# A kernel of two transformer blocks: the first two bunches' expert weights in the order of x's columns, and a 21st slot for expert weights

## The chip, the cores and the metric

The kernel runs on one core of a Trainium2 chip. The metric is the device time of one execution in microseconds, the median of three runs. The engines named here are TensorE (PE, matmuls; PEld is its weight load), VectorE (DVE), ScalarE (ACT), GpSimd (POOL) and SyncE (SP). SyncE issues nearly all loads from device memory to on-chip memory (SBUF), in the order of its program, into one queue that 16 DMA engines serve.

## The reference

Input is x, 256 tokens of 1024 float32 values. The first block is a hybrid of three attention mixers (sliding window with sinks, dilated groups, latent attention), an output projection, a layer norm, and a mixture of experts:

```python
g_logits = x @ w_rg + b_rg                  # 4 groups, the best one is taken
e_logits = (x @ w_re[grp]) + b_re[grp]      # 8 experts in each group, the best two are taken
gate = softmax(top2) * p_grp
y[t] = sum over its 2 experts e: gate * (silu(x[t] @ w_gate[e]) * (x[t] @ w_up[e])) @ w_down[e]
x = layer_norm(ALPHA * x + y, ln2_g, ln2_b)
```

There are 32 experts. `w_gate[e]` and `w_up[e]` are 1024 x 256, `w_down[e]` is 256 x 1024, each 1 MB in float32, so the experts' weights are 96 MB and all of them are read. Behind this come two layers of a second block (differential, grouped-query and memory attention, gates, an output projection and norms), whose weights are 1024 wide too.

The sum over the 1024 rows of `w_gate[e]` may be taken in any order, as long as row i of the weights meets column i of x. This is the freedom that the two layouts below use.

## The kernel before, in words

**Stages.** The input projections and mixers of the first block run until about 177 us of the profile, then the first layer norm and the router until about 201 us, the experts until about 440 us, and the second block behind them.

**Bunches of experts.** The experts go in 8 bunches of 4 (`AT_ONCE`). In each, every expert has 32 places (`PLACES`) for tokens, so the bunch has 128. A 256 x 128 matrix of ones and zeros, `places2`, says which token stands in which place. TensorE gathers the tokens with it: `gather_half` (line 1198) makes for each of 8 chunks k a 128 x 128 result, x's columns of chunk k (stationary) times `places2` (moving), summed over the two halves of the tokens. In the profile a float32 matmul leaves two records, so a half gather is 16 records and a whole one 32. ScalarE copies each half to `q_c` (line 1613). `gate_up` (line 1235 on, matmuls at 1246) then multiplies 32 places of each expert with that expert's gate and up weights, 256 + 256 columns at once, the four experts beside each other; its first half takes chunks 0 to 3, its second chunks 4 to 7. The sigmoid is made by ACT (1619) and DVE (2114 to 2117, `hidden_done`), the hidden values are turned (1224), and `down` (1260) multiplies with the down weights. `add_back` (1232) adds the weighed results to each token's row.

The order on TensorE is: half gather of bunch 0, first half of gate/up of bunch 0, second half gather, second half of gate/up, the residual term (1320, 8 records of 512 columns, only in bunch 0), the whole gather of bunch 1, `down` of bunch 0, `add_back`, gate/up of bunch 1, gather of bunch 2, `down` of bunch 1, and so on.

**Layout of the weights.** Each bunch has 12 items of 1 MB, in this order: four with rows of chunks 0 to 3 of gate and up of its four experts, four with chunks 4 to 7, and four with the down weights. Before the change partition p holds rows 8p to 8p+7 of the gate weights (`(p k) n -> p k n`), so chunk k is every eighth row, and the load moves runs of 4 KB. The gather must then take every eighth column of x as its stationary operand. The down weights are loaded as runs of 8 KB.

**Slots.** An expert item goes into one of 20 slots of 1 MB: the 12 of the tile `ring`, and 8 that lie in other tiles once these are no longer used (`beyond_ring`). `FIRST_SLOTS` is the order in which they are first filled. Four of them (`ONCE`) are filled once only, the others come back at the end of the list each time. `free_for_experts` (from line 707) is what SyncE waits for ahead of each load: for a first filling, the last use by the mixers, the layer norm or the router; later, the use of the item that lies in the slot. `gu_half` b+1 is the end of the first half of gate/up in bunch b, `gu_ready` b+1 that of the second, and `y_ready` 2b+2 the end of its `down`. In bunches 0 to 2 the items and slots are:

- bunch 0: K_C, TILES_MID, BIAS_HIGH, BIAS_LOW, PROBS_T, 2, 3, 4 (gate/up), 0, 1, 6, 9 (down)
- bunch 1: 7, 10, 5, 8, 11, MIX_T, LN_ROWS, X_T (gate/up), then K_C (free at `gu_half` 1), PROBS_T, 2, 3 (at `gu_ready` 1) (down)
- bunch 2: 4 (at `gu_ready` 1), 0, 1, 6, 9 (at `y_ready` 2), 7, 10, 5 (at `gu_half` 2) (gate/up), 8 (at `gu_half` 2), 11, MIX_T, X_T (at `gu_ready` 2) (down)

The last bunch does not use slots 0 to 3; the first weights of the second block (`mem_k0`, `mem_v0`, then `w_in` items 0, 1, 2) are loaded into slots 0 to 4 behind the experts by line 685, in runs of 1 KB. Every load waits in the same queue as the experts' weights.

**Other users of the tiles.** `v_nat` holds the values of two mixers, and `v_c` those of the third; the last product that reads them is the one before the output projection of the first block, `LAST_OUT_1`. During the experts, columns 0 to 1023 of `v_nat` hold the bunch's results (`y_e`). Columns 1024 to 2047 are scratch for the squares of the memory rows (`mem_junk`). `probs` holds the router's values during the experts, in its first columns (`rcol`).

Of the kernel before, what the change touches and what calls it, by code (L numbers as in the profile page):

```python
# [15 lines left out]
P = 128  # L16
# [110 lines left out]
ITEM = {name: n for n, name in enumerate(ITEMS)}  # L127


BIAS_LOW, BIAS_HIGH, PROBS_T, MIX_T, X_T, K_C, TILES_MID, LN_ROWS = range(RING, RING + 8)  # L130
FIRST_SLOTS = (K_C, TILES_MID, BIAS_HIGH, BIAS_LOW, PROBS_T, 2, 3, 4, 0, 1, 6, 9, 7, 10, 5, 8, 11, MIX_T, LN_ROWS, X_T)
ONCE = (TILES_MID, BIAS_HIGH, BIAS_LOW, LN_ROWS)
NEXT_LAYERS = (0, 1, 2, 3)
EXPERT_RING = len(FIRST_SLOTS)
PER_BUNCH = 12


def expert_slots():
# [259 lines left out]
def build(nc, ins, out):  # L398
    ctx = ExitStack()
    with ctx:  # L400
        def sb(name, shape, dt=F32):
            return ctx.enter_context(nc.sbuf_tensor(name, shape, dt))
# [17 lines left out]
        const = sb("const", [P, N_CONST])  # L420
        x_nat = sb("x_nat", [P, 2 * D])
        tiles = sb("tiles", [P, TILES2 * T])
        v_nat = sb("v_nat", [P, 2048])
        q_c = sb("q_c", [P, C_HEADS * T])
        k_c = sb("k_c", [P, C_HEADS * T])
        v_c = sb("v_c", [P, 1024])
        bias = sb("bias", [P, BIAS_HEADS * T])
        probs = sb("probs", [P, 2 * 1152])
        probsT = sb("probsT", [P, 4 * 512])
# [46 lines left out]
        def as_f32(a):  # L476
# [40 lines left out]
        more_g, more_u, more_d = (ring[:, SLOT * k:SLOT * k + SLOT] for k in (9, 10, 11))  # L517
        beyond_ring = {BIAS_LOW: bias[:, 0:2048], BIAS_HIGH: bias[:, 2048:4096], PROBS_T: probsT[:, :],
                       MIX_T: mixT[:, :], X_T: xT[:, :], K_C: k_c[:, :], TILES_MID: tiles[:, 2048:4096],
                       LN_ROWS: tiles[:, 4096:6144]}  # L520

        def expert_slot(n):

# [29 lines left out]
        bucket_sb, rel_sb = probsT[0:N_BUCKETS, 0:VALS + 1], probsT[0:N_BUCKETS, 384:384 + BIAS_HEADS]  # L553
        unseen_sb, bias_sb = probsT[0:BIAS_HEADS, 512:512 + VALS], probsT[0:BIAS_HEADS, 1024:1024 + VALS]
        rope_s = q_c[:, 0:512]
        mem_junk = v_nat[:, 1024:2048]
        rope_a = q_c[:, 7 * T:8 * T]

        def sq_tile(n):
# [11 lines left out]
        def rcol(n):  # L571
            a = rt[0]
            rt[0] += n
            assert rt[0] <= 2048
            return probs[:, a:a + n]

        logitT_sb = rcol(T)
# [74 lines left out]
        def _(sp):  # L652
# [51 lines left out]
            def free_for_experts(n):  # L704

                k = slot_of(n)
                earlier = [m for m in range(FIRST_EXPERT, n) if slot_of(m) == k]
                if earlier:
                    sp.wait_ge(*expert_done(earlier[-1]))
                elif k < MIXERS_RING:  # L710
                    used_up(max(m for m in range(FIRST_EXPERT) if slot_of(m) == k))
                elif k < RING - 1:
                    owners = {UNIT_OWNER[u] for u in range(units_before(OPENING[1])) if u % UNITS // 2 == (k - 5) % 3}
                    sp.wait_ge(p_ready, max(max(users(n)) for n in owners) + 1)
                elif k == K_C:
                    sp.wait_ge(scores, s_first(STEP[("C", 0, C_HEADS - 1)]) + 1)
                elif k == TILES_MID:
                    sp.wait_ge(scores, s_first(STEP[("B", 0, B_HEADS - 1)]) + 3)
                elif k in (BIAS_LOW, BIAS_HIGH):
                    sp.wait_ge(maxed, STEP[("B", 0, B_HEADS - 1)] + 1)  # L720
                elif k == PROBS_T:
                    sp.wait_ge(o_ready, LAST_OUT_1)
                elif k == LN_ROWS:
                    sp.wait_ge(ln_done, 2)
                elif k == X_T:
                    sp.wait_ge(p_ready, JOB[("logit",)] + 1)
                else:
                    sp.wait_ge(p_ready, JOB[("y1", 3, 1)] + 1)

            def load_expert(n):  # L730

                free_for_experts(n)
                b, j = divmod(n - FIRST_EXPERT, PER_BUNCH)
                e = b * AT_ONCE + j % AT_ONCE
                to = expert_slot(n)
                if j < GATE_UP:
                    half = j // AT_ONCE
                    for m, name in enumerate(("w_expert_gate", "w_expert_up")):
                        w = ins[name][0, e].rearrange("(p k) n -> p k n", p=P)
                        sp.dma_start(to[:, SLOT // 2 * m:SLOT // 2 * m + SLOT // 2].rearrange("p (k n) -> p k n", n=DE),  # L740
                                     w[:, 4 * half:4 * half + 4, :]).then_inc(loaded[slot_of(n)], 16)
                else:
                    sp.dma_start(to, ins["w_expert_down"][0, e].rearrange("(p k) n -> p (k n)", p=P)
                                 ).then_inc(loaded[slot_of(n)], 16)
# [99 lines left out]
        def _(pe):  # L844
# [350 lines left out]
                                mm = pe.matmul(o, v, pt[:, T:2 * T], start=False, stop=last)  # L1195
                mm.then_inc(o_ready, 1)

            def gather_half(half):

                dst = bank(4 + half)  # L1200
                for c in range(4):
                    k = 4 * half + c
                    for tt in range(2):
                        mm = pe.matmul(dst[:, P * c:P * c + P],  # L1204
                                       x2[:, tt, :].rearrange("p (q k) -> p k q", k=KC)[:, k, :],
                                       places2[:, tt, :], start=(tt == 0), stop=(tt == 1))
                mm.then_inc(gathered_ready, 1)

            def turn_weighed():
# [2 lines left out]
                    mm = pe.transpose(bank(7)[:, P * tt:P * tt + P], weighed2[:, tt, :], ident)  # L1212
                mm.then_inc(back_ready, 1)

            def gather():

                for half in range(2):
                    gather_half(half)
                turn_weighed()

            def turn_hidden(dst):
# [48 lines left out]
            def more_bunch(n):  # L1270

                i = n + BUNCHES
                pe.wait_ge(placed, i + 1)
                gather()
                pe.wait_ge(gathered_out, 2 * i + 2)
                for e in range(AT_ONCE):
                    pe.wait_ge(more_in, n * (32 * AT_ONCE) + 32 * (e + 1))
# [28 lines left out]
            def experts():  # L1306
# [1 line left out]
                pe.wait_ge(p_dve, taken(JOB[("rank",)]))  # L1308
                pe.wait_ge(setup, 2)
                pe.wait_ge(placed, 1)  # L1310
                gather_half(0)
                for b in range(BUNCHES):
                    gate_up(b, 0)
                    if b == 0:
                        gather_half(1)
                        turn_weighed()
                    gate_up(b, 1)
                    if b == 0:
                        for m in range(4):
                            pe.matmul(bank(m), diagonal[:, P * (m // 2):P * (m // 2) + P],  # L1320
                                      x2[:, m // 2, 512 * (m % 2):512 * (m % 2) + 512],
                                      start=True, stop=False, skip_group_check=True)
                    if b + 1 < BUNCHES:
                        if b > MEM_AT:
                            pe.wait_ge(memT_out, b - MEM_AT)
                        pe.wait_ge(placed, b + 2)
                        gather()
                    else:
                        pe.wait_ge(routed, 1)
                        some = pe.value_load(flags[0:1, 112:113], min_val=0, max_val=1)  # L1330
                    pe.wait_ge(hidden_done, b + 1)
                    turn_hidden(bank(6))
                    pe.wait_ge(hT_out, b + 1)
                    pe.wait_ge(back_out, min(b + 2, BUNCHES))
                    pe.wait_ge(gathered_out, 2 * min(b + 2, BUNCHES))
                    down(b)
                    if MEM_AT <= b < MEM_AT + KC // 2:
                        turn_memory(b - MEM_AT)
                    pe.wait_ge(y0_out, b + 1)
                    pe.wait_ge(y1_out, b + 1)  # L1340
                    add_back(backs[b % 2])
# [1024 lines left out]
```

## Time and profile before

| what | before |
|---|---|
| median of 3 runs | 768.28 us (767.44 to 771.92) |
| the profiled execution | 766.16 us |
| its span, first to last instruction | 764.4 us |
| TensorE busy | 681.9 us, 89% |
| VectorE busy | 368.5 us, 48% |
| ScalarE busy | 324.1 us, 42% |
| DMA | 167.8 MB, mean 220 GB/s |
| mean granted TensorE clock | 0.962 of 2.4 GHz |

The page cuts the span into 40 slices of 19.1 us. These are its rows for the DMA engines:

```
DMA  9967331498667999999999919007263080073301
GB/s 281 339 196 245 111 111 56 127 358 313 247 269 255 416 407 415 413 411 415 410 415 415 322 61 299 29 1 248 83 220 111 1 258 19 1 223 109 111 1 56
```

A digit is the busy share of a slice in tenths. The expert stage is slices 11 to 23, and in its greater part the queue is full at 407 to 416 GB/s. A share over 1 appears where packets of several queues overlap. All times below are of this one execution, from its first instruction.

### The profile page before, as it was taken

To read this page: it belongs to the slowest core of one execution; us is meant where nothing else is said; L and a number is where in the kernel's file an instruction comes from. 1 tells how busy PE (TensorE), PEld (TensorE's weight loads), DVE (VectorE), ACT (ScalarE), POOL (GpSimd) and SP (SyncE) were. 2 spreads that over 40 slices of the span, in tenths; PEclk is the share of its full clock that TensorE was granted. 3 is DMA by queue.
4 is the path that set the end of the run, shared out by engine and by line. 5 is a ranking of instruction groups with operands and counts; after the bars stand their busy time and mean duration, and the time that the engine had idled before them with its cause. 6 is when DMAs were issued, how large, how long until landed. Compare 5 with 4: busy or idle time off the path is not lost.

```text
span 764.4 us, 11653 instructions
## 1 busy us (share of the span) xinstructions
PE 681.9 (89%) x4580; PEld 524.3 (69%) x4582; DVE 368.5 (48%) x813; ACT 324.1 (42%) x759; POOL 16.8 (2%) x31
## 2 busy tenths in 40 slices
PE   6989999996599999697887789999979999999986
PEld 4968998695363555253452378888859898888876
DVE  1633657445431232021110376678775566787743
ACT  2555665421000112120110243578875545788742
POOL 6001000000000000000000000000000000000000
PEclk9999999998599999899999899999999999999999
DMA  9967331498667999999999919007263080073301
GB/s 281 339 196 245 111 111 56 127 358 313 247 269 255 416 407 415 413 411 415 410 415 415 322 61 299 29 1 248 83 220 111 1 258 19 1 223 109 111 1 56
DMA packets 82328, 167.80 MB, mean 220 GB/s; under 512 B 4238, under 2 KB 59264, under 8 KB 78176
## 3 DMA queue, kind: packets, MB, share of 16 engines
q1 hardware_dynamic: 79984, 160.88, 58.1%
q0 software_dynamic: 2160, 6.07, 2.4%
q8 instruction: 39, 0.64, 0.4%
q14 instruction: 17, 0.14, 0.1%
q10 hardware_dynamic: 128, 0.08, 0.0%
HBM read 165.93 MB, written 1.07 MB: 218 GB/s over the span
## 4 chain that ended last, share of the span: by engine, by line
PE 70%; SPq 13%; ACT 5%; DVE 5%; DMA 5%; issue 2%; ACTq 0%; DVEq 0%
PE psum L850 13%; PE psum L852 11%; PE psum L851 11%; SPq L740 9%; PE psum L1204 5%; PE psum L1246 4%; PE psum L893 3%; PE psum L1144 3%; PE psum L1191 2%; DMA ring<-in_w_expert_up_dram 2%; PE psum L1260 2%; SPq L685 2%; DMA ring<-in_w_in_dram 2%; PE psum L1103 2%; PE psum L1232 1%
## 5 line engine op out<-in xcount | busy, mean ns | idle before, releaser
L850 PE MATMUL psum<-a_high,w_high 128*128 128x256 f32 x512 | 150.9, 295 | 2.1 <-ACT q_c L1471 1.3
L851 PE MATMUL psum<-x_low,w_high 128*128 128x256 f32 x512 | 144.6, 283 | 0.0
L852 PE MATMUL psum<-a_high,w_low 128*128 128x256 f32 x512 | 144.6, 283 | 0.0
L2186 DVE TENSOR_TENSOR w_low<-ring,w_high 128x1024 fp32r<-128x1024 f32 (+1 forms) x79 | 111.2, 1422 | 25.1 <-ACT w_high L1571 25.1
L850 PEld LDWEIGHTS psum<-a_high,w_high 128*128 128x128 f32 x512 | 97.7, 191 | 13.9 <-issue 4.7
L1571 ACT ACTIVATE w_high<-ring 128x1024 fp32r<-128x1024 f32 (+1 forms) x79 | 95.9, 1219 | 10.7 <-DMA ring<-in_w_in_dram 7.4
L851 PEld LDWEIGHTS psum<-x_low,w_high 128*128 128x128 f32 x512 | 97.8, 191 | 0.4
L852 PEld LDWEIGHTS psum<-a_high,w_low 128*128 128x128 f32 x512 | 97.8, 191 | 0.0
L1246 PE MATMUL psum<-ring,q_c 128*32 128x512 f32 x368 | 60.7, 654 | 14.6 <-DMA ring<-in_w_expert_up_dram 10.0
L850 PE MATMUL psum<-w_high,a_high 128*128 128x256 f32 x240 | 69.6, 290 | 0.0
L851 PE MATMUL psum<-w_low,a_high 128*128 128x256 f32 x240 | 68.5, 285 | 0.0
L1204 PEld LDWEIGHTS psum<-tiles,x_nat 128*128 128x128 f32 x256 | 61.7, 334 | 8.4 <-issue 8.3
L1204 PE MATMUL psum<-tiles,x_nat 128*128 128x128 f32 x256 | 63.2, 407 | 2.1 <-DVE tiles L2103 2.1
L852 PE MATMUL psum<-w_high,mix_low 128*128 128x256 f32 x192 | 54.8, 286 | 0.0
L2114 DVE TENSOR_SCALAR tiles<-tiles 128x256 f32<-128x256 f32 x8 | 2.3, 292 | 104.8 <-ACT tiles L1619 104.8
L850 PEld LDWEIGHTS psum<-w_high,a_high 128*128 128x128 f32 x240 | 46.7, 195 | 3.2 <-issue 2.3
L1246 PEld LDWEIGHTS psum<-ring,q_c 128*32 128x32 f32 x368 | 15.8, 118 | 46.1 <-issue 46.1
L851 PEld LDWEIGHTS psum<-w_low,a_high 128*128 128x128 f32 x240 | 46.7, 195 | 0.0
L1619 ACT ACTIVATE tiles<-psum 128x256 f32<-128x256 f32 x8 | 3.1, 383 | 100.8 <-PE psum L1246 100.8
L1613 ACT ACTIVATE q_c<-psum 128x512 f32<-128x512 f32 x16 | 9.6, 597 | 69.4 <-PE psum L1204 69.4
L852 PEld LDWEIGHTS psum<-w_high,mix_low 128*128 128x128 f32 x192 | 37.4, 195 | 0.0
L1144 PE MATMUL psum<-const,probs 128*128 128x128 f32 x200 | 31.7, 280 | 4.6 <-DVE probs L1972 2.4
(334 smaller groups left out, 1168.4 us busy)
## 6 DMA issues: line engine op xcount, KB each, us to landing
ring<-in_w_in_dram SPq DMA_DIRECT2D x36, 1024.0 KB, 8.6
ring<-in_w_expert_gate_dram SPq DMA_DIRECT2D x46, 512.0 KB, 14.5
ring<-in_w_expert_up_dram SPq DMA_DIRECT2D x46, 512.0 KB, 15.6
ring<-in_w_expert_down_dram SPq DMA_DIRECT2D x22, 1024.0 KB, 17.4
ring<-in_w_out_dram SPq DMA_DIRECT2D x12, 1024.0 KB, 5.2
ring<-in_w_mem_kv_dram SPq DMA_DIRECT2D x4, 1024.0 KB, 16.8
mixT<-in_w_expert_down_dram SPq DMA_DIRECT2D x3, 1024.0 KB, 18.7
xT<-in_w_expert_down_dram SPq DMA_DIRECT2D x3, 1024.0 KB, 20.6
```

The costliest lines, as they stand in the source:

```text
L685: sp.dma_start(slots[:, s, :, 0:src.shape[2]], src).then_inc(loaded[s], 16)
L740: sp.dma_start(to[:, SLOT // 2 * m:SLOT // 2 * m + SLOT // 2].rearrange("p (k n) -> p k n", n=DE), w[:, 4 * half:4 * half + 4, :]).then_in ...
L850: pe.matmul(dst, left[0], right[0], start=first, stop=False)
L851: pe.matmul(dst, left[0], right[1], start=False, stop=False)
L852: return pe.matmul(dst, left[1], right[0], start=False, stop=last)
L893: mm = pe.matmul(dst, src[:, k, P * tt:P * tt + P], w[:, k, a:b], start=(k == 0), stop=(k == KC - 1))
L1103: mm = pe.matmul(banks[m][:, T * tt:T * tt + T], q[:, P * tt:P * tt + P], k, start=True, stop=True)
L1144: mm = pe.transpose(dst[:, P * c:P * c + P], pr[:, a:a + P], ident)
L1204: mm = pe.matmul(dst[:, P * c:P * c + P], x2[:, tt, :].rearrange("p (q k) -> p k q", k=KC)[:, k, :], places2[:, tt, :], start=(tt == 0), s ...
L1246: mm = pe.matmul(bank(6)[PLACES * e:PLACES * e + PLACES, :], gathered2[b % 2][:, k, PLACES * e:PLACES * e + PLACES], w, start=(k == 0), st ...
L1571: act.activation(split_like_raw(n)[0], raw_of(n), ACT.Copy).then_inc(highs, 1)
L2186: dve.tensor_tensor(w_l, raw_of(n), as_f32(w_h), ALU.subtract).then_inc(lows, 1)
```

## The change

Three things change together.

1. `IN_ORDER = 2`: in bunches 0 and 1, partition p of chunk k holds row 128k + p of the gate and up weights (`(k p) n -> p k n`), so these loads move runs of 1 KB. The gather of these bunches reads `x4`, in which chunk k is 128 neighbouring columns of x. Bunches 2 to 7 and the rounds for more than 32 tokens of an expert keep the old layout. The down weights keep theirs.
2. `v_nat` and `v_c` become parts of one tile, `values`, and its columns 1024 to 3071 are a 21st slot, `V_TOP`. It stands sixth in `FIRST_SLOTS`, behind PROBS_T, waits for the same semaphore as PROBS_T at its first filling, and comes back like the others.
3. `mem_junk` moves from `v_nat` to columns 1152 to 2175 of `probs`, and the router's columns are held below 1152.

With the new list the slots of the first bunches are:

- bunch 0: K_C, TILES_MID, BIAS_HIGH, BIAS_LOW, PROBS_T, V_TOP, 2, 3 (gate/up), 4, 0, 1, 6 (down)
- bunch 1: 9, 7, 10, 5, 8, 11, MIX_T, LN_ROWS (gate/up), X_T, K_C (at `gu_half` 1), PROBS_T, V_TOP (at `gu_ready` 1) (down)
- bunch 2: 2, 3 (at `gu_ready` 1), 4, 0, 1, 6 (at `y_ready` 2), 9, 7 (at `gu_half` 2) (gate/up), 10, 5 (at `gu_half` 2), 8, 11 (at `gu_ready` 2) (down)

```diff
-BIAS_LOW, BIAS_HIGH, PROBS_T, MIX_T, X_T, K_C, TILES_MID, LN_ROWS = range(RING, RING + 8)
-FIRST_SLOTS = (K_C, TILES_MID, BIAS_HIGH, BIAS_LOW, PROBS_T, 2, 3, 4, 0, 1, 6, 9, 7, 10, 5, 8, 11, MIX_T, LN_ROWS, X_T)
+BIAS_LOW, BIAS_HIGH, PROBS_T, MIX_T, X_T, K_C, TILES_MID, LN_ROWS, V_TOP = range(RING, RING + 9)
+FIRST_SLOTS = (K_C, TILES_MID, BIAS_HIGH, BIAS_LOW, PROBS_T, V_TOP, 2, 3, 4, 0, 1, 6, 9, 7, 10, 5, 8, 11, MIX_T, LN_ROWS, X_T)
...
+IN_ORDER = 2
...
-        v_nat = sb("v_nat", [P, 2048])
+        values = sb("values", [P, 3072])
+        v_nat, v_c = values[:, 0:2048], values[:, 2048:3072]
...
-        v_c = sb("v_c", [P, 1024])
...
-                       LN_ROWS: tiles[:, 4096:6144]}
+                       LN_ROWS: tiles[:, 4096:6144], V_TOP: values[:, 1024:3072]}
...
-        mem_junk = v_nat[:, 1024:2048]
+        mem_junk = probs[:, 1152:2176]
...
-            assert rt[0] <= 2048
+            assert rt[0] <= 1152
...
-                elif k == PROBS_T:
+                elif k in (PROBS_T, V_TOP):
                     sp.wait_ge(o_ready, LAST_OUT_1)
...
-                        w = ins[name][0, e].rearrange("(p k) n -> p k n", p=P)
+                        w = ins[name][0, e].rearrange("(k p) n -> p k n" if b < IN_ORDER else "(p k) n -> p k n", p=P)
                         sp.dma_start(to[:, SLOT // 2 * m:SLOT // 2 * m + SLOT // 2].rearrange("p (k n) -> p k n", n=DE),
                                      w[:, 4 * half:4 * half + 4, :]).then_inc(loaded[slot_of(n)], 16)
...
-            def gather_half(half):
+            def gather_half(b, half):
...
-                        mm = pe.matmul(dst[:, P * c:P * c + P],
-                                       x2[:, tt, :].rearrange("p (q k) -> p k q", k=KC)[:, k, :],
-                                       places2[:, tt, :], start=(tt == 0), stop=(tt == 1))
+                        x = x4[:, tt] if b < IN_ORDER else x2[:, tt, :].rearrange("p (q k) -> p k q", k=KC)
+                        mm = pe.matmul(dst[:, P * c:P * c + P], x[:, k, :], places2[:, tt, :],
+                                       start=(tt == 0), stop=(tt == 1))
...
-            def gather():
+            def gather(b):
...
-                gather()
+                gather(BUNCHES)
...
-                gather_half(0)
+                gather_half(0, 0)
...
-                        gather_half(1)
+                        gather_half(0, 1)
...
-                        gather()
+                        gather(b + 1)
```

## Rows read from the trace of the kernel before

**Rows 1.** Windows: span, PE, PEld, DVE, ACT, POOL busy, clock, DMA share, GB/s

```profile
200.00:210.00 10.00, 7.98 (x36) 4.91 (x40) 1.12 (x6) 0.60 (x1) 0.00 (x0) 0.50 0.27 107
...
250.00:420.00 170.00, 143.02 (x847) 76.06 (x847) 29.33 (x61) 23.18 (x49) 0.00 (x0) 0.95 1.02 413
...
236.00:244.00 8.00, 7.09 (x44) 2.50 (x44) 0.69 (x1) 0.00 (x0) 0.00 (x0) 1.00 0.81 244
...
28.00:48.00 20.00, 17.96 (x129) 15.73 (x128) 11.67 (x33) 11.61 (x20) 0.00 (x0) 1.00 1.10 349
...
12.00:16.00 4.00, 4.00 (x10) 3.19 (x11) 2.58 (x3) 1.01 (x2) 0.00 (x0) 1.00 1.14 210
```

**Rows 2.** Chain of waits, in order of time: start us, us, what

```profile
206.20 5.82 PE psum L1246 x32
...
216.71 3.64 PE psum L1246 x32
...
223.98 7.50 PE psum L1204 x32
...
247.65 7.83 PE psum L1204 x32
...
424.73 13.23 DMA ring<-in_w_in_dram
...
440.30 1.22 DVE small L1993 x2
```

**Rows 3.** SyncE's issues in order of time: start us, us, what

```profile
154.19 0.33 SPq L740 DMA_DIRECT2D probsT<-in_w_expert_gate_dram  x1
...
159.91 15.42 SPq L743 DMA_DIRECT2D ring<-in_w_expert_down_dram  x4
...
190.51 0.33 SPq L740 DMA_DIRECT2D xT<-in_w_expert_gate_dram  x1
...
212.09 0.33 SPq L743 DMA_DIRECT2D k_c<-in_w_expert_down_dram  x1
220.41 0.33 SPq L743 DMA_DIRECT2D probsT<-in_w_expert_down_dram  x1
...
236.13 0.33 SPq L740 DMA_DIRECT2D ring<-in_w_expert_gate_dram  x1
...
244.28 0.33 SPq L740 DMA_DIRECT2D ring<-in_w_expert_gate_dram  x1
```

**Rows 4.** Windows of 2 us about the pauses of the DMA engines

```profile
172.00:174.00 2.00, 2.00 (x19) 2.00 (x19) 1.81 (x5) 0.29 (x1) 0.00 (x0) 1.00 0.23 94
...
202.00:204.00 2.00, 2.00 (x10) 2.00 (x10) 0.00 (x0) 0.00 (x0) 0.00 (x0) 0.50 0.33 127
...
232.00:234.00 2.00, 1.57 (x16) 0.55 (x20) 1.04 (x5) 0.38 (x2) 0.00 (x0) 1.00 0.09 37
...
236.00:238.00 2.00, 1.09 (x7) 0.57 (x4) 0.69 (x1) 0.00 (x0) 0.00 (x0) 1.00 0.34 86
```

**Rows 5.** TensorE in order of time: gathers (L1204) and line 1018

```profile
201.33 4.18 PE L1204 MATMUL psum<-tiles,x_nat 128*128 128x128 f32 x16 [2.12 <-DVE tiles L2103]
...
211.95 4.08 PE L1204 MATMUL psum<-tiles,x_nat 128*128 128x128 f32 x16
...
223.82 7.65 PE L1204 MATMUL psum<-tiles,x_nat 128*128 128x128 f32 x32
...
448.31 2.02 PE L1018 MATMUL psum<-diagonal,x_nat 128*128 128x128 f32 x16 [1.55 <-ACT diagonal L1562]
```

**Rows 6.** Weight loads of these lines: ns min/median/max, first and last start

```profile
L1204 PEld LDWEIGHTS psum<-tiles,x_nat x256: 312/335/338, 201.3 to 397.0; 128*128 128x128 f32 x128
...
L1018 PEld LDWEIGHTS psum<-diagonal,x_nat x64: 186/192/192, 448.3 to 607.2; 128*128 128x128 f32 x64
```

**Rows 7.** TensorE in order of time: the router's rank matmuls, five in a row

```profile
196.90 0.60 PE L1009 MATMUL psum<-probs,const 128*128 128x32 f32 x2 [5.47 <-DVE probs L2048]
...
198.60 0.61 PE L1013 MATMUL psum<-probs 128*128 128x32 f32 x2
```

More of the change, by code:

```diff
@@ L1213, in turn_weighed @@
                 mm.then_inc(back_ready, 1)
-            def gather():
+            def gather(b):
                 for half in range(2):
-                    gather_half(half)
+                    gather_half(b, half)
                 turn_weighed()
```

## The prediction, made before the changed kernel was run

> **What bounds the kernel now.** I read four views, in this order: windows by stage, the chain of waits, SyncE's issues in order of time, and TensorE's matmuls in order of time. The expert stage runs from 201 to 440 us, and nothing that the change does shortens a stage before or behind it. So the question is what ends this one.
>
> From 250 to 420 us the DMA engines are never free: share 1.02, 413 GB/s [rows 1]. Before 240 us they often are: share 0.27 from 200 to 210 us. TensorE is the full engine there. The chain says the same in order of time [rows 2]: matmuls from the start of the stage, and at its end the load queue. The last link is a 1 MB load of `w_in`, issued at 424.73 and landed at 437.98 us; its split and the second layer norm follow (440.30). It stands behind all expert weights in one queue. So the stage ends when the queue becomes continuous plus the bytes still to come, and an idle microsecond recovered before that comes off the end.
>
> What ends each idle piece is a slot that comes free [rows 3]. SyncE issues into the last of the 20 slots at 190.51 us, then stands until `gu_half` 1 (212.09), `gu_ready` 1 (220.41), `y_ready` 2 (236.13) and `gu_half` 2 (244.28). The engines run dry at 202.7 (0.33 of a 2 us window) and 232.2 us (0.09), and are filled again at 237.3 (0.34 of the window is used), a microsecond behind the issue [rows 4]. From there they don't stop. TensorE sets all four releases, and before 232 us it spends 4.18 + 4.08 + 7.65 us on gathers [rows 5].
>
> **The change part by part.**
>
> *Gathers of bunches 0 and 1.* The stationary operand becomes 128 neighbouring columns of x in place of every eighth. At the full clock, 16 records (8 matmuls) take 4.08 us now and 32 take 7.65. The same shape from neighbouring columns of the same tile is line 1018's: 16 records in 2.02 us [rows 5], so 32 in about 3.9; its weight load takes 192 ns where the gather's takes 335 [rows 6]. Saved: 2.06 us in the second half of bunch 0, 3.75 us in bunch 1. The first half of bunch 0 runs at 1.2 GHz (granted 0.50 from 200 to 210 us [rows 1]) and takes 4.18/16 = 0.261 us a record. Contiguous ones would take there between 0.213 us, the pace of the rank matmuls ((198.60 − 196.90)/8 [rows 7]), and twice line 1018's 0.126, so the saving is 0.1 to 0.8 us; I take 0.5, the middle. Half of that goes again, because the gate/up matmuls behind then run longer in the slow stretch: 0.25.
>
> The Trainium skill (TensorE: Matmul & The Clock Gate, "Wait — 56ns, not 53.3ns?") gives 106.7 ns cold and 55.6 ns warm for 128 columns, and its page FP8 and Floating Point Precision counts four passes for fp32. An estimate from the two is 3.4 us for the first half and 3.6 us for 16 matmuls, and by it the sum would be 0.7 us larger. No row here shows so quick a gather, and line 1018's pace stands.
>
> Is something else late next? The sigmoid of bunch 0 takes 4.2 us from the end of gate/up to `hidden_done`; TensorE has 3.6 us of residual and 3.9 us of gather over it, so it stays hidden. If it did not, what it exceeds them by would come back. The copies to `q_c` stay behind each half gather. So `gu_half` 1 comes 0.25 us earlier, `gu_ready` 1 2.3 us (0.25 + 2.06), `y_ready` 2 6.05 us (2.3 + 3.75): 230.1 us. `gu_half` 2 moves as far, to 238.2.
>
> *The 21st slot* waits for the same semaphore as PROBS_T (154.19 us [rows 3]), so no new wait stands in SyncE's queue. Every item behind it takes the slot one place earlier. At 190.51 us the ninth item of bunch 1 goes out instead of the eighth, and the load that `y_ready` 2 releases is one further on. One MB at 413 GB/s [rows 1] is 2.54 us less behind that point.
>
> *1 KB runs for 4 KB in the 16 gate/up items of bunches 0 and 1.* A full queue of 1 KB runs moves 349 GB/s, one of expert weights 413 [rows 1]: 3.00 against 2.54 us per MB, 7.4 us in all. Where do they fall? From 154.2 us: four gate/up items (12.0), one down item (2.5), two more (5.1), to 173.8 us. Today the queue runs empty near 172.5 us [rows 4], while SyncE stands within its four down issues until 175.3 us, for a slot of the mixers [rows 3]; that pause is filled. Then a down and a gate/up item (5.5), six gate/up items from 177.4 (18.0), LN_ROWS (3.0), X_T as a down item (2.5): empty at about 204 us, 202.7 before. The next release is at 212, so the 7.4 us are paid where nobody waits, with 8 to spare. Bunch 1's last gate/up item lands near 202 us and is wanted at 238. SyncE issues two loads per item as before.
>
> *From 212 us on.* K_C and the memory rows last to 218; `gu_ready` 1 at 218.1 releases four items, done at about 229.8; `y_ready` 2 at 230.1 four more, flowing from 231.3; `gu_half` 2 (238.2) comes before those are through (241.5). Later releases lead by as much as today. The continuous stretch starts at 231.3 instead of 237.3.
>
> *The rest costs nothing.* The values keep their places within one tile; the squares' scratch moves to columns of `probs` that the router does not use. The third `w_in` load's slot is now freed by the last down product, which in today's trace ends near 430.5 us, where SyncE comes to that load; the critical one is the second.
>
> **Sum.** 6.0 (earlier start) + 2.54 (one MB fewer) = 8.5 us. All of it passes to the end, because TensorE needs 23.7 us from gather to gather (223.98 to 247.65 [rows 2]) and the queue 12 × 2.54 = 30.5 us per bunch. The span goes from 764.4 to 755.9 us, the profiled run from 766.2 to 757.7; the median of the runs, 768.28, is 2.1 above that run: 759.8 us.
>
> Bounds: the first gather's 0.1 to 0.8, and the poor rate of a burst, 244 GB/s at share 0.81 over 236 to 244 us [rows 1], some 2 us that a queue already running may not lose, or may lose once more: 6.5 to 10.5 us saved, 757.8 to 761.8.
>
> **Rivals.**
>
> *The clock comes back later.* It returns to 2.4 GHz after about 9 us of work, inside the gate/up matmuls that take 5.82 us on the chain, against 3.64 for as many at the full clock [rows 2]. A shorter gather brings the copy's gap forward. Should the return come after these matmuls, they take 2 × 3.64 = 7.3 (1.4 more), and some of the next gather is slow (0.6): 761.8 us. For it: the return lies close behind the changed work. Against: TensorE is busy on both sides of a 0.65 us gap, as now. 0.17.
>
> *The layout does not speed the gather*, because the load is bound by something else. Only the slot is left: 765.7 us. Against it, line 1018 reads the very same tile. 0.07.
>
> *1 KB runs go far slower (the slower side).* Its place is the queue from 154 to 231 us. The lowest row with such runs has 210 GB/s, among small loads (12 to 16 us [rows 1]), and 4 KB bursts fall to 244. Twelve gate/up items lie behind 154.2 us, with five down items (12.7) and then six more MB (15.2) before `y_ready` 2. The queue is late from 4.1 us per item on, 256 GB/s. At 210 GB/s it is 5.0: 154.2 + 60 + 27.9 = 242.1, 10.8 us behind, and the net is 2.3 us slower, 770.6; at 190 GB/s 777. Against: 20 us at 349. 0.06, half of it past +1%.
>
> The Trainium skill (DMA: Bandwidth & Descriptors, "Why small descriptors are slow (HBM only)") counts a fixed 3 cycles per packet, by which an estimate for 1 KB against 4 KB is 7% more time. The rows show 18%, and they are used; by either the queue is idle at 212 us.
>
> *More than forecast:* the burst loses nothing and the gather has its best bound: 757.5 us. 0.10.
>
> **Chances.** Forecast 0.60, rivals as given. About 1%, 7.7 us, is what a measurement of this kernel can tell from no change, so the line is 760.6 us and runs through the forecast's own range. Faster by over 1%: 0.42 of the forecast's 0.60, and the 0.10: 0.52. Slower 0.03, within 1% 0.45. The range is 756.8 to 765.5: it takes in the bounds, the late clock and, nearly, the slot alone.
>
> **What would show it.** Right: gather records at 0.126 us in the first two bunches and 0.245 in the others; issues near 218 and 230 us; a full queue from 231 us; the second `w_in` load landed near 429.5, and all that follows 8 to 9 us early. Wrong: a queue still full at 212 us, 1 KB items below 300 GB/s, 1.2 GHz beyond 212 us, or TensorE waiting for bunch 1's weights.

## The result, and the profile after

| what | before | changed |
|---|---|---|
| median, first comparison | 767.74 us (10 runs) | 759.57 us (10 runs) |
| ratio, first comparison | | 0.9888, 95% interval 0.9862 to 0.9915 |
| ratio, second comparison (kernel a1, the same code) | | 0.9916, 95% interval 0.9885 to 0.9947 |
| span of the profiled execution | 764.4 us | 760.2 us; a1: 754.8 us |

The kernel became about 1% faster, 6.4 to 8.6 us by the two comparisons. The forecast was 8.5 us and 759.8 us. The prediction's line between "faster by over 1%" and "within 1%", 760.6 us, runs between the two measured medians (759.57 and 760.96 us): the two comparisons fall on either side of it. The first profile of the changed kernel alone would mislead: its span is only 4.2 us shorter. The second one is 9.6 us shorter. So two profiles of the same code are read here beside the one of before. Lines of the changed kernel have moved by one or two: the gather is L1206 (before L1204), `gate_up` L1247 (L1246), `down` L1261 (L1260), the residual L1321 (L1320).

First the chain of waits of the changed kernel's first profile, from the first gather on, and the end of its expert stage (columns: start us, us, what):

```profile
204.95 3.77 PE psum L1206 x16
...
209.39 5.57 PE psum L1247 x32
214.96 2.00 PE psum L1206 x16
...
217.63 3.64 PE psum L1247 x32
221.27 3.63 PE psum L1321 x8
224.90 3.58 PE psum L1206 x32
...
229.43 3.69 PE psum L1261 x32
...
244.65 7.83 PE psum L1206 x32
...
424.50 3.67 PE psum L1233 x8
428.17 3.20 issue
431.37 1.07 PE psum L1352 x3
```

The gathers of bunches 0 and 1 answer to [rows 5]: 2.00 us in place of 4.08, 3.58 in place of 7.5 on the chain, and bunch 2's is 7.83 as ever. But the stage begins at 204.95 us, 3.6 us later than before, and near its end stand 3.20 us in which TensorE waits for nothing that the profile shows. Neither was in the prediction.

The same stretch in a1, TensorE in order of time:

```profile
201.45 3.76 PE L1206 MATMUL psum<-tiles,x_nat 128*128 128x128 f32 x16 [2.12 <-DVE tiles L2104]
...
211.83 2.05 PE L1206 MATMUL psum<-tiles,x_nat 128*128 128x128 f32 x16
...
221.68 3.73 PE L1206 MATMUL psum<-tiles,x_nat 128*128 128x128 f32 x32
```

Here the stage begins where it began before (201.33 [rows 5]). SyncE's issues in a1, which answer to [rows 3]:

```profile
211.97 0.34 SPq L744 DMA_DIRECT2D k_c<-in_w_expert_down_dram  x1
218.27 0.33 SPq L744 DMA_DIRECT2D probsT<-in_w_expert_down_dram  x1
...
230.08 0.33 SPq L741 DMA_DIRECT2D ring<-in_w_expert_gate_dram  x1
...
238.22 0.33 SPq L741 DMA_DIRECT2D ring<-in_w_expert_gate_dram  x1
```

Forecast were about 211.8, 218.1, 230.1 and 238.2 us. And the windows of a1 (columns as in [rows 1]):

```profile
206.00:208.00 2.00, 2.00 (x12) 0.48 (x16) 0.00 (x0) 0.00 (x0) 0.00 (x0) 0.50 0.06 16
212.00:214.00 2.00, 2.00 (x18) 1.86 (x18) 0.00 (x0) 0.08 (x1) 0.71 (x1) 1.00 0.58 74
...
226.00:228.00 2.00, 1.62 (x16) 0.55 (x20) 0.99 (x5) 0.32 (x2) 0.00 (x0) 1.00 0.92 231
228.00:230.00 2.00, 2.00 (x20) 0.39 (x12) 0.00 (x0) 0.60 (x1) 0.00 (x0) 1.00 0.98 356
230.00:232.00 2.00, 1.09 (x6) 0.63 (x4) 0.69 (x1) 0.00 (x0) 0.00 (x0) 1.00 0.91 348
232.00:234.00 2.00, 2.00 (x6) 0.81 (x5) 0.00 (x0) 0.00 (x0) 0.00 (x0) 1.00 0.87 219
...
180.00:200.00 20.00, 9.95 (x44) 7.13 (x44) 9.41 (x41) 2.88 (x7) 0.00 (x0) 0.67 1.10 350
...
250.00:420.00 170.00, 143.99 (x834) 71.50 (x838) 30.84 (x62) 22.82 (x50) 0.00 (x0) 0.91 1.02 411
```

The queue with 1 KB runs moves 350 GB/s from 180 to 200 us and is empty at 206.1 us. (Its share of 1.10 is that of one queue alone, 110.1% for SyncE's, and it was 109.8% from 28 to 48 us in [rows 1]: with 1 KB runs a share over 1 does not take several queues.) It is busy again from 212.8 us, and the pause that the old kernel had from 232 to 237 us [rows 4] is gone. The critical `w_in` load was used at 437.98 us in the kernel before. In a1, ScalarE's line for it and DVE's for the layer norm behind it are:

```profile
428.12 1.06 ACT L1572 ACTIVATE w_high<-ring 128x1024 fp32r<-128x1024 f32 x1 [0.88 <-DMA ring<-in_w_in_dram]
...
430.35 1.29 DVE L1994 BATCH_NORM_STATS2 small<-psum 128x6 f32<-128x512 f32 x2
```

Both are 9.9 us earlier than before (437.98 and 440.21 there). But not all of it passes on. Two things must be done before TensorE can turn the normed rows (the scaled transposes, L1018 before, L1019 now): the layer norm behind the `w_in` load, and TensorE's own work, which is the last bunch's `down` and `add_back`, the first matmuls of the second block (L986) and those of line 894. Before, TensorE was done first and waited 1.55 us for the layer norm [rows 5]. In a1 it does not wait, and the chain of waits runs through its own work:

```profile
424.44 3.67 PE psum L1233 x8
...
431.16 5.12 PE psum L986 x23
436.29 3.47 PE psum L894 x16
```

```profile
439.58 1.95 PE L1019 MATMUL psum<-diagonal,x_nat 128*128 128x128 f32 x16
```

The transposes start 8.7 us earlier than before (448.31 to 439.58 us). What is behind them takes 315.2 us in place of 316.1, and the span is 9.6 us shorter.

### The profile page after: what moved, and what is told of

Read it like the earlier page. It is cut to its first block, busy times and chain, and to the rows that moved or that the text cites. A ratio compares the mean times of both kernels' runs of the same rounds, so it can differ in the third digit from the quotient of the medians.

```text
span 760.2 us, 11653 instructions
## 1 busy us (share of the span) xinstructions
PE 682.1 (90%) x4580; PEld 520.5 (68%) x4582; DVE 368.4 (48%) x813; ACT 324.3 (43%) x759; POOL 16.8 (2%) x31
## 4 chain that ended last, share of the span: by engine, by line
PE 72%; SPq 11%; DMA 5%; ACT 5%; DVE 4%; issue 2%; ACTq 0%; DVEq 0%
PE psum L851 13%; PE psum L853 11%; PE psum L852 11%; SPq L741 9%; PE psum L1206 4%; PE psum L1247 4%; PE psum L894 4%; PE psum L1145 3%; DMA ring<-in_w_expert_down_dram 3%; PE psum L1261 3%; PE psum L1192 2%; DMA ring<-in_w_expert_up_dram 2%; PE psum L986 2%; PE psum L1104 2%; PE psum L1233 1%
## 5 line engine op out<-in xcount | busy, mean ns | idle before, releaser
L1247 PE MATMUL psum<-ring,q_c 128*32 128x512 f32 x320 | 55.1, 682 | 11.0 <-DMA ring<-in_w_expert_up_dram 7.0
L1206 PEld LDWEIGHTS psum<-tiles,x_nat 128*128 128x128 f32 x256 | 55.2, 307 | 9.1 <-issue 9.1
L1206 PE MATMUL psum<-tiles,x_nat 128*128 128x128 f32 x256 | 56.9, 382 | 2.1 <-DVE tiles L2104 2.1
L1247 PEld LDWEIGHTS psum<-ring,q_c 128*32 128x32 f32 x320 | 13.6, 123 | 42.5 <-issue 42.5
```

Source lines behind the costliest of these rows:

```text
L1206: mm = pe.matmul(dst[:, P * c:P * c + P], x[:, k, :], places2[:, tt, :], start=(tt == 0), stop=(tt == 1))
L1247: mm = pe.matmul(bank(6)[PLACES * e:PLACES * e + PLACES, :], gathered2[b % 2][:, k, PLACES * e:PLACES * e + PLACES], w, start=(k == 0), st ...
```

## The experiments

The kernels of one group share a chip and the runs of the kernel before; group b ran on another chip than a and c. The a kernels and c1 have 11 or 12 runs each, b1 four, the others six. The kernel before without edits had medians of 767.47, 768.15 and 767.25 us in the groups a, b and c.

**a1: the changed kernel again.** No edit.

> The changed kernel again, nothing else. In its first profile it entered the experts 3.6 us later than the kernel before (first gather at 204.95 against 201.33 us), and after the last add_back TensorE's branch over the extra rounds took 6.55 us against 0.47, with 3.2 us of idle TensorE. Theory 1: the late entry is the granted clock's own luck (slow stretches of 6.8 and 10.2 us before 201 us against 3.4 and 6.8), so it differs here, while from first gather to y_ready 2 it again takes 28.2 us, give or take 1. Theory 2: the change itself delays the mixers and the router through its 1 KB loads: then the entry is at 204 to 206 us again with no more slow clock than before. The long branch: if it belongs to the kernel it is there again, 5 to 7 us; if it is chance it is below 1. Ratio to before 0.986 to 0.992.

Median 760.96 us, ratio 0.9916 (0.9885 to 0.9947), on the edge of what was expected. Theory 1 holds. The late start is the clock's: these are the windows of 182 to 193 us in the first profile, and then in a1.

```profile
182.00:193.00 11.00, 8.54 (x28) 5.14 (x29) 1.54 (x2) 2.39 (x4) 0.00 (x0) 0.53 1.10 350
```

```profile
182.00:193.00 11.00, 7.64 (x34) 4.92 (x34) 2.09 (x11) 2.39 (x4) 0.00 (x0) 0.78 1.10 348
```

Granted was 0.53 against 0.78, with the same queue on full load in both. The router's matmuls there took 5.92 us on the chain in place of 3.63. Another 1.3 us were lost in the mixers at 141 to 149 us (0.57 against 0.79). That slow stretch began while the load queue was still empty: granted 0.91 from 140 to 142 us, with a DMA share of 0.00 until 144 us. From first gather to `y_ready` 2 it is 28.2 us in the first profile (204.95 to 233.1) and 28.6 in a1; before it was 34.8. The branch differs between two executions of the same code. In the first profile:

```profile
L1344 PEldq COMPARE_BRANCH  x1: 6554/6554/6554, 424.5 to 424.5; - x1
```

and in a1:

```profile
L1344 PEldq COMPARE_BRANCH  x1: 472/472/472, 424.5 to 424.5; - x1
```

So it is not the code alone that makes it long.

**a2: only the slot.**

```diff
-IN_ORDER = 2
+IN_ORDER = 0
```

> Only the 21st slot: IN_ORDER = 0, so the old layout, loads and gathers in all bunches. Theory 1: one MB at 413 GB/s less behind the start of the continuous stretch, 2.5 us faster than before, ratio 0.9967; y_ready 2 about 34.8 us after the first gather, as before. Rival: the slot gives nothing, because the extra item only fills a pause of which another is left: ratio 1.000. Second rival: the slot is the whole gain, ratio 0.989.

Median 762.75 us, ratio 0.9961 (0.9929 to 0.9993): 3.0 us (0.5 to 5.4), expected 2.5. The gathers and releases are the old ones. The stage's layer norm:

```profile
436.51 1.29 DVE L1994 BATCH_NORM_STATS2 small<-psum 128x6 f32<-128x512 f32 x2
```

That is 3.7 us earlier than before, while `y_ready` 2 came at 235.9 as ever. The slot's MB is gained behind it. Here TensorE still waits for the layer norm, 1.49 us, and the whole gain reaches the end: the span is 3.8 us shorter (760.6 us). Both rivals, no gain and the whole gain, lie outside the interval.

**a3: only the order of the first two bunches**, with 20 slots.

```diff
-FIRST_SLOTS = (K_C, TILES_MID, BIAS_HIGH, BIAS_LOW, PROBS_T, V_TOP, 2, 3, 4,
+FIRST_SLOTS = (K_C, TILES_MID, BIAS_HIGH, BIAS_LOW, PROBS_T, 2, 3, 4,
```

> Only the order of the first two bunches (1 KB loads and gathers of neighbouring columns), with the 20 slots of before. Theory 1: 6.0 us faster than before, ratio 0.992; gather records at 0.122 to 0.126 us in bunches 0 and 1, y_ready 2 about 28.2 us after the first gather. Rival: the 1 KB loads take part of it, 3 us or less are left, ratio 0.996 or more.

Median 764.38 us, ratio 0.9942 (0.9907 to 0.9976): 4.4 us (1.8 to 7.1). The expected 6.0 lies in the interval, and so does 3; by the ratio alone the rival is not excluded. Its profile has the late start and the long branch (6.54 us). From first gather to `y_ready` 2 it is 28.2 us as forecast, and the layer norm is at 435.90, 231.0 us behind the first gather at 204.94, where the old kernel needs 238.9 (440.21 − 201.33): 7.9 us. So inside the stage the gain is there, and part of it is given back at the stage's end and behind it. Here too the chain runs through TensorE's own work at the end.

**a4: only the 1 KB loads.** As a3, and the gather strided, so the products of the first two bunches pair wrong rows and columns.

```diff
-                        x = x4[:, tt] if b < IN_ORDER else x2[:, tt, :].rearrange("p (q k) -> p k q", k=KC)
+                        x = x2[:, tt, :].rearrange("p (q k) -> p k q", k=KC)
```

> Only the 1 KB loads: bunches 0 and 1 have their gate and up rows in the new order, but the gather stays strided, so the products of these two bunches pair rows and columns wrongly; 20 slots. It prices the loads. Theory 1 (they are paid while nobody waits): same as before within 1 us, ratio 0.999 to 1.001, and the queue is empty before gu_half 1. Rival: they delay the router, the first bunch or the queue: 2 to 7 us slower than before, ratio 1.003 to 1.010.

Median 768.04 us, ratio 1.0006 (0.9980 to 1.0033). The loads cost nothing that can be measured, at most 2.5 us. The layer norm stands 238.3 us behind the first gather (442.14 − 203.85), against 238.9. The queue is empty from 206 us (DMA share 0.00) until `gu_half` 1 at 214.2, as expected. Theory 1 holds.

**b1: all bunches in order.**

```diff
-IN_ORDER = 2
+IN_ORDER = 8
```

> The changed kernel with IN_ORDER = 8: all bunches have 1 KB loads and gathers of neighbouring columns. It prices a 1 KB run where the queue is full. Theory 1: the 48 further gate/up items cost 3.00 in place of 2.54 us each and TensorE's faster gathers there only wait longer: 22 us slower than the changed kernel, 13.5 us slower than before, ratio 1.018. Rival: runs of 1 KB move as fast as 4 KB once the queue is full, and the whole is the changed kernel's time, ratio 0.989.

Median 778.31 us, ratio 1.0164 (1.0104 to 1.0223). The queue from 250 to 420 us:

```profile
250.00:420.00 170.00, 119.88 (x755) 50.08 (x753) 26.27 (x52) 21.12 (x45) 0.00 (x0) 0.84 1.07 370
```

It is as full as in a1 and moves 370 GB/s in place of 411, with two thirds of its bytes in 1 KB runs. This is what the same runs cost when somebody waits. Against a1 the medians differ by 17.4 us for 48 items (778.31 − 760.96), 0.36 us each, but the two ran on different chips. By the ratios, each to the kernel before on its own chip, it is 19 to 21 us, 0.40 to 0.44 each (1.0164 against 0.9916 and 0.9888). The 0.46 taken was about right. TensorE is busy 120 us of the 170 in place of 144; its faster gathers bring nothing here. The rival is excluded.

**b2: without the branch over the extra rounds** (left out: rounds for experts with more than 32 tokens), on the engines `sp`, `pe`, `act` and `dve`.

```diff
-                with pe.If(some):
+                if False:
```

> The changed kernel without the branch over the extra rounds on all four engines (the rounds for experts with more than 32 tokens are left out). Two of the three profiles so far with the new gathers had a branch of 6.5 us on TensorE behind the last add_back, the third one and the three with the old gathers 0.5. Theory 1: the long branch costs 3 us in some executions, so this kernel is 1 to 2 us faster than the changed one on average, ratio to before 0.987 to 0.989, and its idle TensorE behind the last add_back is below 0.5 us. Rival: the w_in load and its split end the stage anyway, and the time is the changed kernel's within 0.5 us.

Median 755.93 us (754.14 to 757.39), ratio 0.9845 (0.9806 to 0.9884). By the ratios that is 3.3 and 5.5 us below the two results of the changed kernel, more than the 1 to 2 expected; but the interval overlaps the expected 0.987 to 0.989. The six runs spread by 3 us only, the 10 and 11 of the changed kernel by 10 and 8. In its profile TensorE has no pause behind the last `add_back`, and the layer norm is again what the transposes wait for:

```profile
437.22 2.02 PE L1019 MATMUL psum<-diagonal,x_nat 128*128 128x128 f32 x16 [1.03 <-ACT diagonal L1563]
```

So the rival had the chain right (the `w_in` load and its split end the stage) and the time wrong: it took the same chain for the changed kernel, where in both profiles TensorE ends last.

**c1: the kernel before without that branch** (left out: the same rounds). The same edit in the old kernel.

> The kernel before, without the branch over the extra rounds on all four engines (left out: rounds for experts with more than 32 tokens). Without it the changed kernel took 755.9 us in place of 759.6 to 761.0. Theory 1: the long branch comes with the changed kernel only (3 of 4 profiles without other edits of TensorE's order; never with the old gathers), and cost it some 3.5 us: here the gain is 0 to 1 us, ratio 0.998 to 1.000. Rival: both kernels have it in a part of their executions, and the old one gains as much, ratio 0.995.

Median 765.05 us, ratio 0.9974 (0.9948 to 1.0001), 2 us. It stands between theory and rival, and does not tell them apart. Without the branch on both sides, the change is 0.9845/0.9974 = 0.9871, some 10 us (6 to 13 by the two intervals), close to the 9.6 of the profile with a short branch.

**b3: the residual matmuls in the router's pause.** In the changed kernel the four residual matmuls of bunch 0 stand before the gather of bunch 1. b3 moves them behind the logits.

```diff
                 elif kind == "rank":
...
+                    for m in range(4):
+                        pe.matmul(bank(m), diagonal[:, P * (m // 2):P * (m // 2) + P],
+                                  x2[:, m // 2, 512 * (m % 2):512 * (m % 2) + 512],
+                                  start=True, stop=False, skip_group_check=True)
                     pe.wait_ge(chosen_done, 1)
```

> The changed kernel with bunch 0's four residual matmuls (3.63 us on the path before y_ready 2) moved into TensorE's idle time between the logits and the rank matmuls. Theory 1 (the stage ends by when the queue becomes continuous): y_ready 2 comes 3.6 us earlier, but gu_ready 1 does not, and the four items it frees fill the queue until 229 us; only the last gap of 1 to 2 us is recovered, 1 to 2 us faster than the changed kernel, ratio to before 0.986 to 0.989. Rival A: every microsecond on TensorE's path counts, 3.6 us, ratio 0.984 to 0.986. Rival B: TensorE's work at 191 to 197 us also keeps the clock at 2.4 GHz, the first gather and gate/up run fast, all releases come 3 to 4 us earlier: 4 to 6 us faster than the changed kernel, ratio 0.982.

Median 754.50 us, ratio 0.9841 (0.9791 to 0.9890). 5 us below the changed kernel's first median, but the interval takes in theory 1 and both rivals, so the time does not tell them apart. `y_ready` 2 stands 25.4 us behind the first gather in place of 28.6. The slow clock here is 0.57 over 200 to 210 us, against 0.50.

**b4: the same with zeros in the rest of the pause.** Twelve matmuls of zeros beside it.

```diff
+                    for m in range(5):
+                        pe.matmul(bank(4), zeros_b[:, 0:P], zeros_b[:, :], start=True, stop=True)
                     pe.wait_ge(chosen_done, 1)
...
+                for m in range(7):
+                    pe.matmul(bank(4), zeros_b[:, 0:P], zeros_b[:, :], start=True, stop=True)
                 pe.wait_ge(p_dve, taken(JOB[("rank",)]))
```

> As b3, with twelve matmuls of zeros beside it (5 before the rank matmuls, 7 behind, into a free bank) so that TensorE works nearly without a pause from 191 to 201 us. Theory 1: the slow clock from 193.5 to 210.6 us is owed to the idle router stretch, so it now goes or shortens, the first gather takes 2.0 and gate/up 3.7 us, and the releases come 3 to 4 us earlier: 4 to 6 us faster than the changed kernel, ratio 0.981 to 0.984. Rival: it does not, and the zeros in a slow stretch delay the rank matmuls by 1 to 4 us: as slow as the changed kernel or slower.

Median 755.02 us, ratio 0.9829 (0.9788 to 0.9871). Windows of b4:

```profile
190.00:200.00 10.00, 8.16 (x36) 4.30 (x38) 7.75 (x42) 0.41 (x2) 0.00 (x0) 1.00 1.10 349
200.00:210.00 10.00, 8.85 (x81) 4.59 (x84) 2.00 (x10) 1.19 (x2) 0.71 (x1) 1.00 0.73 268
```

The clock stays at 2.4 GHz where before it was 1.2 from 193.5 us on. The first half gather takes 2.04 us on the chain and gate/up behind it 3.64, in place of 3.77 and 6.01. Its layer norm comes at 421.47 us, 8.9 us before a1's. But the span is 750.7 us, only 4.1 us less than a1's. Of the 4.8 us between, 1.7 went at the stage's end, where TensorE's own work ends last (the transposes start at 432.42 us, 7.2 before a1's), and 3.1 in the second block, which takes 318.3 us behind them in place of 315.2. A stretch of slow clock lies there (granted 0.65 from 550 to 560 us).

**c2: zeros alone.** 29 matmuls of zeros in the changed kernel, 22 before the rank matmuls and 7 behind; the residual in its old place.

> The changed kernel with 29 matmuls of zeros in TensorE's idle time of the router (22 before the rank matmuls, 7 behind), the residual matmuls in their old place. Theory 1: the zeros alone lift the slow clock of 193 to 210 us, so gu_half 1, gu_ready 1 and y_ready 2 all come 4 us earlier than in the changed kernel (226 us) and the time falls by 3 to 4 us, ratio 0.985. Rival: only real work counts, or the stretch stays, and the time is the changed kernel's, ratio 0.989 to 0.992.

Median 756.21 us, ratio 0.9848 (0.9813 to 0.9884). Windows of c2:

```profile
200.00:210.00 10.00, 8.61 (x74) 5.12 (x78) 1.23 (x6) 1.19 (x2) 0.71 (x1) 1.00 0.52 190
210.00:220.00 10.00, 10.00 (x69) 5.92 (x62) 6.34 (x24) 0.98 (x2) 0.00 (x0) 1.00 0.93 369
```

Work that computes nothing keeps the clock up and is worth 3 to 5 us here. `y_ready` 2 is at 224.8 us, 5.3 us before a1's. Theory 1 holds.

**c3: b4 again.**

> b4 again: its profile had y_ready 2 at 220.6 us and the second layer norm at 421.4 us, 8.9 us before the changed kernel's best profile, but its span was only 4.1 us shorter, since a slow clock stretch of 10.2 us lay at 553 us in the second block. Theory 1: that stretch is the clock's luck in one execution; here the second block takes 324 us again and the span is 746 to 748, with a median of 752 to 756 over the runs. Rival: the stretch belongs to the kernel and is there again.

Median 755.46 us, ratio 0.9827 (0.9786 to 0.9867), b4's value twice. The slow stretch was not there (1.00 from 550 to 560 us), and the second block took 315.3 us behind the transposes: the same code can have it or not. But the span is 754.0, not 746 to 748: this execution had the long branch. Its chain:

```profile
415.60 3.67 PE psum L1239 x8
419.27 2.93 issue
422.21 0.60 PE psum L1355 x2
422.81 2.33 issue
425.14 1.01 PE psum L1355 x2
```

5.3 us of idle TensorE stand at the stage's end, and the slow clock follows. The same place of b4:

```profile
418.69 0.05 issue
418.75 0.38 PE psum L1355
419.13 2.51 issue
421.63 0.59 PE psum L1355 x2
422.22 6.91 PE psum L986 x32
```

The second gap is in both, so it is no price of the long branch; the first, 2.93 us, is c3's alone. Line 986, the first matmuls of the second block, took 6.91 us here and 9.24 us in c3.

**c4: b4 without the branch** (left out: the extra rounds).

> b4 without the branch over the extra rounds (left out: rounds for experts with more than 32 tokens). Theory 1: gains add up. b4's profile had a short branch, but other executions may not: 751 to 754 us, ratio 0.979 to 0.982. Rival: with the queue full almost from 206 us on, the w_in load and its split end the stage and the branch no longer counts: b4's time within 1 us.

Median 750.47 us (749.77 to 751.91), ratio 0.9780 (0.9747 to 0.9814), 5 us under b4 and c3. The gains add up, and more: the runs lie within 2.2 us, and the median is just below the 751 to 754 expected. In its profile neither of c3's two gaps is there, and the layer norm is again what the transposes wait for (0.29 us). So the second gap may belong to the branch too, though it does not need a long one; one profile of c4 does not settle it.

## Why the prediction was right, step by step

*The gathers.* Right in size. The record's pace in a1 is 0.128 us for the half gather (2.05/16) and 0.117 us for the whole one (3.73/32), against the 0.122 to 0.126 of line 1018. Saved were 2.0 and 3.9 us, forecast 2.06 and 3.75. The first half gather at 1.2 GHz took 3.76 us in place of 4.18, 0.4 us against the 0.5 taken, and half of that was lost in the matmuls behind (6.01 against 5.82 us), as said. That last part is one profile's: in the first they took 5.57 us.

*The releases.* Within 0.2 us of all four in a1. From first gather to `y_ready` 2 the step was 6.2 us (34.8 to 28.6), forecast 6.05.

*The slot.* Forecast 2.5, measured alone 3.0 us (0.5 to 5.4), and 3.7 in its profile at the layer norm.

*The 1 KB runs.* Their place was right: alone they cost nothing (a4), and in the full queue they cost 0.36 to 0.44 us an item (b1). The empty queue was at 206.1 us, forecast 204. The forecast's rate of 349 GB/s is the one measured.

*The queue from 212 us.* Here a term was too small. I had the engines run dry between 229.8 and 231.3 us. They did not: the four items before were moved at poor rates (231 GB/s at 226 to 228 us) and lasted until the next came. The layer norm moved by 9.9 us in a1, not by 8.5. Of the 1.4 us, the 1.5 us gap that did not open is what I can place; that the poor rate costs nothing net is not shown.

*The sum.* Forecast 8.5 us, measured 6.4 to 8.6. It agrees, but in part by luck: two errors stand against each other. The layer norm gained more than forecast, 9.9 us in a1. And one step of the prediction was wrong: "All of it passes to the end". It compares TensorE's and the queue's pace within the bunches, and leaves out who is last at the stage's end. There TensorE's own work had a slack of 1.55 us only, the wait of the first L1018 in [rows 5]. A gain of 9.9 us at the `w_in` load is more than TensorE's work followed with: it came 7.0 us earlier in a1 (end of `add_back` 435.13 to 428.11 us), and with the slack the transposes came 8.7 us earlier. The last bunch's gate/up took 6.53 us there, in part at the slow clock, and 5.34 before.

Once TensorE is last, every pause on it counts. Some executions had one at the stage's end, in the branch over the extra rounds: 6.5 us of branch in place of 0.5, beside 3.7 us of `add_back`, so 3 us of idle, and then slow clock in the first matmuls of the second block. From the layer norm to the scaled transposes before and a1 need 8.1 and 9.2 us, the first profile of the changed kernel 11.6, b4 11.0, c3 15.8. No step of the prediction had this.

*Rivals.* The late clock did not happen: in a1 the clock returned 9.3 us behind the first gather, as before, and in the first profile 8.4 us behind it. That profile's 3.6 us were lost ahead of the stage. The layout does speed the gather (a3). The far slower 1 KB runs did not come.

**What stays open:** why the branch is long in some executions. It was long in five of eight profiles with the new gathers (first profile, a3, b1, c2, c3), and in none of three with the old ones (before, a2, a4). With one profile each this is no proof that the change brings it, and c1 leaves room for 0 to 4 us in the old kernel. One thing parts the profiles: in the five with the long branch TensorE had sat idle 0.78 to 2.36 us just before the last `down`, waiting for its weights; in the six with the short one 0.47 us for ScalarE, or 0.61 us for the weights (a4). That is a correlation over eleven profiles, and no run tests it.

The best complete kernel by the ratios is b4: 0.9829 and 0.9827 in two groups, some 13 us faster than before and about 5 us faster than the changed one. b3 (0.9841) and c2 (0.9848) lie within its interval.

## What to carry to other kernels

Where one queue is full for most of a stage, look for the moment at which it becomes full for good: what TensorE does before it is worth its time in full, and an operation that is expensive behind it (1 KB runs: 0.36 to 0.44 us per MB) can be free before it. Read two profiles of the same code before you explain a few microseconds: two stretches of slow clock moved a whole stage by 3.6 us here. And ask at the place where two chains meet how much slack the one has that ends first: here it was 1.55 us, the gain at the other was 9.9, and from then on every pause of TensorE counted, with a branch that left it idle for 3 us in some executions.

## What the runs showed of the hardware that was not expected

- A float32 weight load of 128 columns, every eighth, takes 335 ns, and of neighbouring ones 186 to 192 ns. The records' pace is 0.245 and 0.12 us.
- Twenty-nine matmuls of zeros in the router's pause kept the granted clock at 1.00 over 200 to 210 us, where it was 0.50 without them; four real ones of float32 gave 0.57.
- One and the same branch instruction took 0.47 us or 6.5 us, and nothing between: 6554, 6542, 6550, 6578 and 6510 ns in five profiles, 359 to 472 in six.
- A queue of 4 and 8 KB runs moved 411 to 413 GB/s over 170 us on one core; two thirds of it in 1 KB runs 370, all of it 349. The Trainium skill (DMA: Bandwidth & Descriptors, "Specifications") gives 512 B as the least transfer for line rate. These traces do not agree: at 1 KB it is 85% of the rate.
